# Moving the gate's exponentials on ScalarE, and the weights' lower half and the gating product on VectorE, in a projection stage

## The chip, the cores and the metric

The kernel runs on one core of a Trainium2 chip. Its time is the device time of one launch in microseconds; the median of three runs of the kernel before is 3620.22 us (3617.70 to 3620.62).

## What is computed

Two blocks follow each other on a sequence of 1024 tokens of width 1024: a gated MLP mixer and a dilated attention, then a block that mixes stick-breaking attention, a state-space recurrence (SSD) and a gated linear recurrence, and ends in an MLP. The change lies in the input projection of the second block, cut here to what matters:

```
h    = concat(16 meta tokens, x)                      # 1040 tokens
proj = rmsnorm(h) @ w_in                              # units of 128 features
xbc  = silu(causal_conv(proj[x,B,C], 4 taps) + bias)  # 8 units
z, q, g of the recurrences = silu(proj[z,q,g])        # 8 units
log_keep = log_sigmoid(-q k), summed from the right; w = exp(log_sigmoid(q k) + sum)
```

silu(y) is computed as y * exp(-ln(1 + exp(-y))), so that one activation table serves: ScalarE does Exp, Ln and Exp in place in one tile, `ce`, and VectorE multiplies.

## The kernel before

All matrix products of the projection are done in float32 by splitting each operand into a rounded upper part and a lower rest, and adding three products. ScalarE makes the upper half of a weight tile (`split_hi`, L137), VectorE the rest (`split_lo`, L142), and TensorE multiplies (`products`, L155) after it has waited for the lower half (`split`, L146).

`projection_and_sticks` (from L2492) works through 27 units of 128 output features, u = 0 to 26. A unit has three pieces, j = 0, 1, 2, of 352, 344 and 344 tokens (`PIECES`). Each piece has 8 groups of three matmuls into its own PSUM bank g[j]; TensorE may start piece (u, j) when VectorE has evicted piece (u-1, j). Weight tiles alternate between two buffers by u % 2. Units 7 to 14 go through the convolution (`is_x`), 15 to 22 only through silu (`is_silu`); both are "gated". Units 23 to 26 are stored raw.

The order of the work is written out by hand. `drive` calls, on every engine, `piece(p)` for p = 3u + j, `slot(c)` and `phase(k)`:

- pieces 6 to 14 (units 2 to 4) by themselves;
- 57 slots (c = -1 to 55) of stick-breaking attention. In slot c TensorE computes the scores of step c+1 (L2918, L2921), the sums of step c (L2931, L2933), the values of step c-1 (L2902), and then 6 or 7 groups of the projection, numbers 360c/56 to 360(c+1)/56. ScalarE and VectorE run the slot's own work first (ScalarE: L2767, L2769, L2771, then L2777, L2780, L2786; VectorE: L3103, L3112, L3117, L3121), and then the pieces that TensorE ends in that slot (units 5 to 19);
- 31 phases of the SSD recurrence, with the pieces of units 20 to 26 behind them in the same way.

Each engine works through its queue in order, so a wait in a piece holds up the next slot of that engine. Within `piece`, before the change:

- ScalarE: at j = 1 `split_hi` for the next unit, then (unit u-1 gated) a wait for VectorE's clamped tile (`s_cm`) and the first Exp (L2742); at j = 2 Ln (L2745) and the second Exp (L2747).
- VectorE: at j = 1 `split_lo` for the next unit; the eviction (L2996), which waits until TensorE has ended this piece; at j = 0 `finish(u-2)`, the gating product (L3011); then for unit u-1 two taps of the convolution at j = 0 (L3074, L3076), two more at j = 1 (L3080) and the clamp into `ce` (L3083; for silu units L3089 only). The clamp waits for the gating product of the unit before it.
- SyncE: at j = 1 the weights of unit u+2 are loaded (L132) and unit u-2 is stored (L2629).

Of the kernel before, what the change touches and what calls it, by code (L numbers as in the profile page):

```python
# [17 lines left out]
ACT = mybir.ActivationFunctionType  # L18
# [45 lines left out]
def wait(eng, sem, value):  # L64

    if isinstance(value, int) and value <= 0:
        return
    eng.wait_ge(sem, value)
# [2423 lines left out]
def projection_and_sticks(nc, a, w, hi, lo, inv, x, x_again, x_out, over_x, heads, hg, keep, table, cst, proj, conv, o_cat, ident, ones):  # L2492
# [10 lines left out]
    NU = len(units)  # L2503
# [5 lines left out]
    gated = lambda u: is_x(u) or is_silu(u)  # L2509
    n_gated = lambda u: u - 7  # L2510
# [13 lines left out]
    with Stage(nc, "pr") as st:  # L2524
# [17 lines left out]
        ce = st.sb("ce", [P, LM])  # L2542
# [152 lines left out]
        def _(act):  # L2695
# [20 lines left out]
            def root(u):  # L2716
                i = qk.index(u)
                act.wait_ge(s_pb, 3 * u + 3)
                nc.scalar.activation(cy[i % 2][:, :], cy[i % 2][:, :], ACT.Exp, scale=-0.5).then_inc(s_r, 1)

            def piece(p):
                u, j = p // 3, p % 3
                if j == 0 and u - 3 in qk:
                    root(u - 3)
                if j == 1 and u + 1 < NU:
                    w.split_hi(act, (u + 1) % 2, (u + 1) // 2, free=(s_mm, 3 * (u - 1) + 3))
                if u - 2 in qk:
                    i = qk.index(u - 2)
                    if j == 0:
                        act.wait_ge(s_ev, 3 * (u - 2) + 3)  # L2730
                        wait(act, s_blk, 3 * i)
                        nc.scalar.activation(ce[:, :], ev[(u - 2) % 3][:, TAPS - 1:], ACT.Square).then_inc(s_psq, 1)
                    c0, c1 = PIECES[j]
                    act.wait_ge(s_blk, 3 * i + j + 1)
                    if j == 0:
                        wait(act, s_nrm, i - 1)
                    nc.scalar.activation(cy[i % 2][:, c0:c1], pb[:, 0:c1 - c0], ACT.Ln, bias=eps[:, :], scale=1.0 / HD).then_inc(s_pb, 1)
                if gated(u - 1):
                    n = n_gated(u - 1)
                    if j == 1:  # L2740
                        act.wait_ge(s_cm, n + 1)
                        nc.scalar.activation(ce[:, :], ce[:, :], ACT.Exp, scale=-1.0).then_inc(s_cx, 1)  # L2742
                    if j == 2:
                        act.wait_ge(s_cx, n + 1)
                        nc.scalar.activation(ce[:, :], ce[:, :], ACT.Ln, bias=1.0).then_inc(s_cl, 1)  # L2745
                        act.wait_ge(s_cl, n + 1)
                        nc.scalar.activation(ce[:, :], ce[:, :], ACT.Exp, scale=-1.0).then_inc(s_ce, 1)  # L2747
                if (u, j) == (DT + 2, 0):
                    act.wait_ge(s_sdp, 64)
                    nc.scalar.activation(par[:, 2:3], par[:, 1:2], ACT.Exp).then_inc(s_dte, 1)  # L2750
                    act.wait_ge(s_dt, 2)
                    nc.scalar.activation(tmp, tmp, ACT.Exp, scale=-1.0).then_inc(s_dte, 1)
                    act.wait_ge(s_dte, 2)
                    nc.scalar.activation(tmp, tmp, ACT.Ln, bias=1.0).then_inc(s_dte, 1)
                if (u, j) == (DT + 4, 0):
                    act.wait_ge(s_dtc, 5)
                    for name in ("ecum", "wend", "elast"):
                        nc.scalar.activation(keep[name], keep["cum" if name == "ecum" else name], ACT.Exp).then_inc(s_dtx, 1)

            def slot(c):  # L2760
# [26 lines left out]
                for p in in_slot(c):  # L2787
                    piece(p)
# [28 lines left out]
            def phase(k):  # L2817
# [11 lines left out]
                if k == hg_from + 6:  # L2829
                    factors(0)  # L2830
            drive(act, piece, slot, phase)

        @block.tensor
# [117 lines left out]
        def _(dve):  # L2951
# [38 lines left out]
            def evict(u, j):  # L2990
                c0, c1 = PIECES[j]
                src = begin[u][j] if u < 2 else g[j]
                dve.wait_ge(s_mm, 3 * u + j + 1)
                if is_raw(u - 3):
                    dve.wait_ge(s_rawout[u % 3], 16 * raw_uses(u))
                nc.vector.tensor_tensor(ev[u % 3][:, TAPS - 1 + c0:TAPS - 1 + c1], src[:, 0:c1 - c0], inv[:, c0:c1], ALU.mult).then_inc(s_ev, 1)  # L2996
# [11 lines left out]
            def finish(u):  # L3008
                dve.wait_ge(s_ce, n_gated(u) + 1)
                src = cy[u % 2][:, :] if is_x(u) else ev[u % 3][:, TAPS - 1:]  # L3010
                nc.vector.tensor_tensor(cy[u % 2][:, :], src, ce[:, :], ALU.mult).then_inc(s_out, 1)  # L3011

            def piece(p):
                u, j = p // 3, p % 3
                if j == 1 and u + 1 < NU:
                    w.split_lo(dve, (u + 1) % 2, (u + 1) // 2)
                if j == 0 and u - 3 in qk:
                    i = qk.index(u - 3)
                    dve.wait_ge(s_scaled, 1)
# [2 lines left out]
                                                   cy[i % 2][:, :], ALU.mult, ALU.mult).then_inc(s_nrm, 1)  # L3022
                    dve.wait_ge(s_nrm, i + 1)
                evict(u, j)
                if (u, j) == (DT + 1, 1):
                    dve.wait_ge(s_kept, 16 * KT)
                    dve.wait_ge(s_sdp, 64)
                    dve.wait_ge(s_ev, 3 * u)
                    nc.vector.memset(dtf[:, 0:P - META], 0.0)
                    nc.vector.memset(tmp[:, 0:P - META], 0.0)  # L3030
                    nc.vector.tensor_scalar(dtf[:, P - META:], ev[DT % 3][0:SSD_HEADS, TAPS - 1:], par[:, 0:1], None, ALU.add).then_inc(s_dt, 1)
                    dve.wait_ge(s_dt, 1)
                    nc.vector.scalar_tensor_tensor(tmp[:, P - META:], dtf[:, P - META:], -1.0, dtf[:, P - META:], ALU.mult, ALU.max).then_inc(s_dt, 1)
# [17 lines left out]
                if u - 2 in vs:  # L3051
# [10 lines left out]
                            nc.vector.tensor_copy(vt[i][:, 4:8, :], src).then_inc(s_pb, 1)  # L3062
                    else:
                        nc.vector.tensor_copy(vt[i][:, 8, :], pb[:, 0:P]).then_inc(s_pb, 1)
                if j == 0 and gated(u - 2):
                    finish(u - 2)
                if is_x(u - 1):
                    v, n = u - 1, n_gated(u - 1)
                    src = ev[v % 3]
                    y = cy[v % 2][:, :]  # L3070
                    if j == 0:
                        wait(dve, s_gone[v % 2], 16 * (n // 2))
                        dve.wait_ge(s_ev, 3 * u)
                        nc.vector.tensor_scalar(y, src[:, 0:LM], taps[:, n, 0:1], cbias[:, n:n + 1], ALU.mult, ALU.add).then_inc(s_cc, 1)  # L3074
                        dve.wait_ge(s_cc, 4 * n + 1)
                        nc.vector.scalar_tensor_tensor(y, src[:, 1:1 + LM], taps[:, n, 1:2], y, ALU.mult, ALU.add).then_inc(s_cc, 1)  # L3076
                    if j == 1:
                        for t in (2, 3):
                            dve.wait_ge(s_cc, 4 * n + t)
                            nc.vector.scalar_tensor_tensor(y, src[:, t:t + LM], taps[:, n, t:t + 1], y, ALU.mult, ALU.add).then_inc(s_cc, 1)  # L3080
                        dve.wait_ge(s_cc, 4 * n + 4)
                        wait(dve, s_out, n)
                        nc.vector.tensor_scalar(ce[:, :], y, LOWEST, None, ALU.max).then_inc(s_cm, 1)  # L3083
                if is_silu(u - 1) and j == 1:
                    v, n = u - 1, n_gated(u - 1)
                    wait(dve, s_gone[v % 2], 16 * (n // 2))
                    dve.wait_ge(s_ev, 3 * u)
                    wait(dve, s_out, n)
                    nc.vector.tensor_scalar(ce[:, :], ev[v % 3][:, TAPS - 1:], LOWEST, None, ALU.max).then_inc(s_cm, 1)  # L3089

            def slot(c):
# [50 lines left out]
                for p in in_slot(c):  # L3142
                    piece(p)
# [41 lines left out]
            def phase(k):  # L3185
# [18 lines left out]
                if k == hg_from + 7:  # L3204
# [5 lines left out]
                    nc.vector.tensor_tensor(hg["kend"][0][:, :, :], hg["kend"][0][:, :, :], key[:, :, :], ALU.mult).then_inc(h_done, 1)  # L3210
                    dve.wait_ge(h_done, 1)
            drive(dve, piece, slot, phase)
    w.passed((14, 13), (0, 0))

# [935 lines left out]
```

## Time and profile before

| | |
|---|---|
| median of three runs | 3620.22 us (3617.70 to 3620.62) |
| the profiled execution | 3614.36 us |
| its span, first to last instruction | 3612.6 us |
| projection stage, units 2 to 26 | 2065 to 2598 us of the span |
| TensorE busy | 3451.5 us (96%) |
| VectorE busy | 2170.2 us (60%) |
| ScalarE busy | 1537.2 us (43%) |

Times in the rows are microseconds from the start of the span. A matmul's end is modelled: matmuls are pipelined, so in an unbroken run each starts about 0.16 us before the modelled end of the one before it. The idle time before an instruction stands in square brackets with what released it. TensorE's granted clock is given as a share of 2.4 GHz.

### The profile page before, as it was taken

Reading aid. Unit: us, or ns where it says so; the run is one execution under the profiler, and the core shown is the slowest. Engines: PE = TensorE matmul, PEld = TensorE weight load, DVE = VectorE, ACT = ScalarE, POOL = GpSimd, SP = SyncE. Lnnn points to the kernel's source line nnn. Section 1 sums busy time; section 2 is a strip of 40 time slices with the busy share of each in tenths; the row PEclk is TensorE's granted clock in tenths of the full one; section 3 lists DMA queues with packets and bytes.
Section 4 is the critical chain, followed back from the end, with each engine's and each line's share of the span. In section 5 each row is a group of like instructions: output and inputs, shape, how many; then the busy total and the mean of one; then the engine's idle time right before and its main releaser. Section 6 shows DMA issues by size and latency. Waiting matters only on the chain. (4 is left out here: it accounts for less than half of the span.)

```text
span 3612.6 us, 48153 instructions
## 1 busy us (share of the span) xinstructions
PE 3451.5 (96%) x17578; PEld 2817.6 (78%) x17578; DVE 2170.2 (60%) x4264; ACT 1537.2 (43%) x3062; POOL 121.9 (3%) x151
## 2 busy tenths in 40 slices
PE   8999999989999999999999799999879989999999
PEld 6878887867777777777777687778867877878887
DVE  5477773575555666666675646656666566644443
ACT  4254453445444454544444445555224322232222
POOL 0000001000000000000000200000000000000000
PEclk9999999999999999999999999999989999999999
DMA  4232225622111221222233300112232222322223
GB/s 147 94 106 92 88 91 187 193 68 62 59 59 55 65 66 63 68 65 64 67 100 123 124 28 32 50 56 77 96 108 91 96 86 72 108 93 94 99 94 123
DMA packets 162585, 316.84 MB, mean 88 GB/s; under 512 B 33744, under 2 KB 79360, under 8 KB 162224
## 3 DMA queue, kind: packets, MB, share of 16 engines
q1 hardware_dynamic: 144432, 268.49, 22.5%
q0 software_dynamic: 15808, 36.89, 3.3%
q10 hardware_dynamic: 2112, 8.39, 0.6%
q8 instruction: 142, 2.33, 0.3%
q14 instruction: 91, 0.75, 0.1%
HBM read 260.22 MB, written 59.71 MB: 89 GB/s over the span
## 5 line engine op out<-in xcount | busy, mean ns | idle before, releaser
L142 DVE TENSOR_TENSOR all_w_lo<-all_w_raw,all_w_hi 128x1024 fp32r<-128x1024 f32 x241 | 295.1, 1225 | 256.8 <-ACT all_w_hi L137 256.8
L137 ACT ACTIVATE all_w_hi<-all_w_raw 128x1024 fp32r<-128x1024 f32 x241 | 253.5, 1053 | 454.8 <-PE om_z L155 261.5
L155 PE MATMUL om_z<-all_hi,all_w_hi 128*128 128x512 f32 x640 | 256.9, 401 | 7.5 <-DVE all_w_lo L142 4.3
L155 PE MATMUL om_z<-all_hi,all_w_lo 128*128 128x512 f32 x640 | 255.1, 399 | 0.0
L155 PE MATMUL om_z<-all_lo,all_w_hi 128*128 128x512 f32 x640 | 253.6, 396 | 0.0
L2122 DVE CUSTOM_DVE_ANT_0 at_logit<-da_qk,at_bias 128x256 f32<-128x256 f32 (+1 forms) x384 | 130.1, 377 | 164.2 <-issue 163.6
L155 PE MATMUL pr_g<-all_hi,all_w_hi 128*128 128x344 f32 (+1 forms) x624 | 217.7, 349 | 11.4 <-PEq L45 4.9
L1668 ACT ACTIVATE at_p<-at_logit,da_pair_max 128x256 f32<-128x256 f32 (+1 forms) x384 | 177.5, 465 | 100.3 <-DVE da_pair_max L2122 100.3
L1660 ACT ACTIVATE at_pt<-da_tr 128x512 f32<-128x512 f32 (+1 forms) x192 | 101.2, 527 | 263.6 <-PE da_tr L1860 263.4
L155 PE MATMUL pr_g<-all_hi,all_w_lo 128*128 128x344 f32 (+1 forms) x624 | 206.4, 331 | 0.0
L155 PE MATMUL pr_g<-all_lo,all_w_hi 128*128 128x344 f32 (+1 forms) x624 | 205.2, 329 | 0.0
L155 PE MATMUL om_z<-om_h_hi,all_w_hi 128*128 128x512 f32 x512 | 202.3, 395 | 1.7 <-DVE all_w_lo L142 1.7
L155 PE MATMUL om_z<-om_h_lo,all_w_hi 128*128 128x512 f32 x512 | 200.1, 391 | 0.0
L155 PE MATMUL om_z<-om_h_hi,all_w_lo 128*128 128x512 f32 x512 | 200.0, 391 | 0.0
L3968 DVE TENSOR_TENSOR all_yo<-all_yo,om_z 128x512 f32<-128x512 f32 x80 | 55.0, 687 | 183.4 <-PE om_z L155 183.3
L1870 PE MATMUL da_pv<-at_v,at_pt 128*128 128x64 f32 x1280 | 164.1, 267 | 0.0
L1870 PEld LDWEIGHTS da_pv<-at_v,at_pt 128*128 128x128 f32 x1280 | 159.8, 192 | 1.9
L2139 DVE TENSOR_TENSOR da_o<-da_pv,da_rden 128x128 f32<-128x128 f32 x192 | 56.0, 292 | 167.4 <-PE da_pv L1870 161.8
L155 PEld LDWEIGHTS om_z<-all_hi,all_w_hi 128*128 128x128 f32 x640 | 121.9, 190 | 36.9 <-DVE all_w_lo L142 4.5
L1196 ACT ACTIVATE all_w_hi<-all_w_raw 128x512 fp32r<-128x512 f32 x190 | 118.3, 623 | 72.4 <-PE da_by L1214 23.8
L3863 ACT ACTIVATE om_h_hi<-om_m 128x512 fp32r<-128x512 f32 x64 | 40.4, 632 | 254.5 <-DVE om_m L3966 254.5
L155 PEld LDWEIGHTS om_z<-all_lo,all_w_hi 128*128 128x128 f32 x640 | 121.6, 190 | 27.8
(827 smaller groups left out, 8908.0 us busy)
## 6 DMA issues: line engine op xcount, KB each, us to landing
all_w_raw<-in_w_mlp SPq DMA_DIRECT2D x128, 512.0 KB, 3.4
all_w_raw<-in_w_qkv SPq DMA_DIRECT2D x136, 256.0 KB, 2.7
all_w_raw<-in_w_ug SPq DMA_DIRECT2D x48, 512.0 KB, 4.1
all_w_raw<-in_w_in SPq DMA_DIRECT2D x27, 512.0 KB, 3.5
all_w_raw<-in_w_v SPq DMA_DIRECT2D x20, 512.0 KB, 4.6
vhat<-ag_vst ACTq DMA_DIRECT2D x4, 2048.0 KB, 7.4
ow_v<-vhat SPq DMA_DIRECT2D x16, 512.0 KB, 3.4
da_before<-o_groups POOLq DMA_DIRECT2D x32, 256.0 KB, 3.9
```

What stands on the lines that cost most here:

```text
L137: self.nc.scalar.activation(self.hi[b][:, :], self.raw[b][:, :], ACT.Copy).then_inc(self.hi_done[b], 1)
L142: self.nc.vector.tensor_tensor(self.lo[b][:, :], self.raw[b][:, :], self.hi[b][:, :].bitcast(F32), ALU.subtract).then_inc(self.lo_done[b], 1)
L155: last = self.nc.tensor.matmul(out, wp[b][:, w], ap[:, k, cols], start=(k == 0 and m == 0), stop=(k == KT - 1 and m == 2))
L1196: self.nc.scalar.activation(self.hi[n % self.slots], self.tile[name], ACT.Copy, scale=self.scales[j] if name in ("a11", "a12") else 1.0).t ...
L1660: nc.scalar.activation(pt[t % 2][:, 0:wd], tr[:, 0:wd], ACT.Copy).then_inc(s_pt, 1)
L1668: last = nc.scalar.activation(p[t % 2][:, hh, 0:wd], logit[t % 2][:, hh, 0:wd], ACT.Exp, scale=-1.0, bias=pair_max[:, t, hh:hh + 1], accum ...
L1870: last = nc.tensor.matmul(pv[:, 64 * hh:64 * hh + 64], pt[t % 2][:, i * P:i * P + P], v[:, t + x, 64 * hh:64 * hh + 64], start=(x == 0), s ...
L2122: last = nc.vector.tensor_tensor_reduce(out=logit[t % 2][:, hh, 0:wd], in0=qk[hh][:, 0:wd], in1=bias[ag][hh][x][:, :], scale=1.0, scalar=3 ...
L2139: nc.vector.tensor_tensor(o[:, t, :].rearrange("p (h c) -> p h c", h=2), pv[:, 0:P].rearrange("p (h c) -> p h c", h=2), rden[:, t, :].rear ...
L3863: nc.scalar.activation(h_hi[:, i, :], m[n % 2][:, :], ACT.Square)
L3968: nc.vector.tensor_tensor(x[:, i, halves[h]], x[:, i, halves[h]], z[b][:, :], ALU.add).then_inc(s_ev, 1)
```

## The change

On ScalarE the first Exp moves from (u, 1) to (u, 2), where Ln follows it, and the second Exp from (u, 2) to (u+1, 0). On VectorE `split_lo` for the next unit moves from in front of the eviction of (u, 1) to behind the eviction of (u, 2), and in (u, 0) `finish(u-2)` moves behind the first two taps. No instruction is added or removed.

```
 scalar, piece(p):
-                if gated(u - 1):
+                if gated(u - 1) and j == 2:
                     n = n_gated(u - 1)
-                    if j == 1:
-                        act.wait_ge(s_cm, n + 1)
-                        nc.scalar.activation(ce[:, :], ce[:, :], ACT.Exp, scale=-1.0).then_inc(s_cx, 1)
-                    if j == 2:
-                        act.wait_ge(s_cx, n + 1)
-                        nc.scalar.activation(ce[:, :], ce[:, :], ACT.Ln, bias=1.0).then_inc(s_cl, 1)
-                        act.wait_ge(s_cl, n + 1)
-                        nc.scalar.activation(ce[:, :], ce[:, :], ACT.Exp, scale=-1.0).then_inc(s_ce, 1)
+                    act.wait_ge(s_cm, n + 1)
+                    nc.scalar.activation(ce[:, :], ce[:, :], ACT.Exp, scale=-1.0).then_inc(s_cx, 1)
+                    act.wait_ge(s_cx, n + 1)
+                    nc.scalar.activation(ce[:, :], ce[:, :], ACT.Ln, bias=1.0).then_inc(s_cl, 1)
+                if gated(u - 2) and j == 0:
+                    n = n_gated(u - 2)
+                    act.wait_ge(s_cl, n + 1)
+                    nc.scalar.activation(ce[:, :], ce[:, :], ACT.Exp, scale=-1.0).then_inc(s_ce, 1)
 vector, piece(p):
-                if j == 1 and u + 1 < NU:
-                    w.split_lo(dve, (u + 1) % 2, (u + 1) // 2)
...
                 evict(u, j)
+                if j == 2 and u + 1 < NU:
+                    w.split_lo(dve, (u + 1) % 2, (u + 1) // 2)
...
-                if j == 0 and gated(u - 2):
-                    finish(u - 2)
                 if is_x(u - 1):
...
+                if j == 0 and gated(u - 2):
+                    finish(u - 2)
                 if is_silu(u - 1) and j == 1:
```

## Rows read from the trace of the kernel before

**Rows 1.** The page: span, busy time by engine, clock in 40 slices.
```profile
span 3612.6 us, 48153 instructions
PE 3451.5 (96%) x17578; PEld 2817.6 (78%) x17578; DVE 2170.2 (60%) x4264; ACT 1537.2 (43%) x3062; POOL 121.9 (3%) x151
PEclk9999999999999999999999999999989999999999
```

**Rows 2.** Windows by stretch: length, each engine's busy time (instructions), clock, DMA share, GB/s.
```profile
2106.00:2181.00 75.00, 71.76 (x389) 58.02 (x388) 39.29 (x79) 44.88 (x89) 0.00 (x0) 0.98 0.07 24
2181.00:2390.00 209.00, 188.98 (x999) 153.91 (x999) 140.41 (x232) 120.11 (x223) 0.00 (x0) 0.92 0.12 41
2390.00:2475.00 85.00, 83.10 (x470) 68.59 (x468) 48.05 (x90) 54.61 (x99) 1.84 (x2) 0.99 0.19 66
2475.00:2598.00 123.00, 112.69 (x739) 109.98 (x738) 85.53 (x151) 41.91 (x78) 7.93 (x11) 0.99 0.27 91
```

**Rows 3.** TensorE's waits, 2106 to 2473 us: total us, times, longest.
```profile
PE pr_zb L2918 <- ACT pr_wt L2777: 17.4, 9, 3.7
PE pr_zb L2931 <- DVE ox_sticks L3121: 4.6, 6, 1.5
```

**Rows 4.** All waits, 2181 to 2390 us: ScalarE's longest.
```profile
ACT pr_ce L2742 <- DVE pr_ce L3083: 43.9, 8, 7.5
```

**Rows 5.** Timeline around the first of them: start, duration, engine, operation, idle before.
```profile
2200.80 1.07 ACT L2742 ACTIVATE pr_ce<-pr_ce 128x1040 f32<-128x1040 f32 x1 [7.53 <-DVE pr_ce L3083]
2202.94 0.26 ACT L2777 ACTIVATE pr_wt<-pr_zb 128x128 f32<-128x128 f32 x1
2203.26 1.22 PE L2918 MATMUL pr_zb<-hs_heads 64*128 64x384 f32 x2 [2.10 <-ACT pr_wt L2777]
```

**Rows 6.** TensorE's waits, 2473 to 2598 us.
```profile
PE pr_zb L2354 <- ACT pr_sp L2387: 3.5, 1, 3.5
```

**Rows 7.** Two lines, 2064 to 2598 us: count, duration in ns, min/median/max.
```profile
L142 DVE TENSOR_TENSOR all_w_lo<-all_w_raw,all_w_hi x25: 1202/1224/1226, 2063.6 to 2575.1; 128x1024 fp32r<-128x1024 f32 x25
L2996 DVE TENSOR_TENSOR pr_ev<-pr_g,all_inv x75: 491/516/527, 2071.6 to 2597.9; 128x344 f32<-128x344 f32 x50, 128x352 f32<-128x352 f32 x25
```

**Rows 8.** Timeline, start of unit 2.
```profile
2063.21 0.51 DVE L2996 TENSOR_TENSOR pr_ev<-pr_ob,all_inv 128x344 f32<-128x344 f32 x1
2063.63 1.22 DVE L142 TENSOR_TENSOR all_w_lo<-all_w_raw,all_w_hi 128x1024 fp32r<-128x1024 f32 x1
2064.95 0.63 PE L155 MATMUL pr_g<-all_hi,all_w_hi 128*128 128x352 f32 x1 [4.93 <-issue]
```

**Rows 9.** Timeline, end of unit 3 and start of unit 4.
```profile
2093.10 0.32 PE L155 MATMUL pr_g<-all_lo,all_w_hi 128*128 128x344 f32 x1
2093.46 0.52 DVE L2996 TENSOR_TENSOR pr_ev<-pr_g,all_inv 128x344 f32<-128x344 f32 x1 [3.84 <-PE pr_g L155]
2093.58 0.58 PE L155 MATMUL pr_g<-all_hi,all_w_hi 128*128 128x352 f32 x1
```

**Rows 10.** Timeline, end of unit 10: two groups' ends, next unit's start, eviction.
```profile
2253.02 0.32 PE L155 MATMUL pr_g<-all_lo,all_w_hi 128*128 128x344 f32 x1
2253.49 0.32 PE L155 MATMUL pr_g<-all_lo,all_w_hi 128*128 128x344 f32 x1
2253.65 0.32 PE L155 MATMUL pr_g<-all_hi,all_w_hi 128*128 128x352 f32 x1
2261.44 0.51 DVE L2996 TENSOR_TENSOR pr_ev<-pr_g,all_inv 128x344 f32<-128x344 f32 x1
```

**Rows 11.** Timeline of a slot in which nobody is late.
```profile
2183.75 1.03 PE L2918 MATMUL pr_zb<-hs_heads 64*16 64x512 f32 x2
2186.54 0.41 PE L155 MATMUL pr_g<-all_hi,all_w_hi 128*128 128x352 f32 x1
2188.36 0.67 DVE L3121 TENSOR_TENSOR ox_sticks<-pr_sp,pr_sp_hi 16x512 fp32r<-16x512 f32 x1
```

**Rows 12.** Windows from a gap on TensorE on: three of twelve.
```profile
2115.60:2121.80 6.20, 3.97 (x14) 3.69 (x14) 2.44 (x6) 2.59 (x5) 0.00 (x0) 0.73 0.00 0
2280.60:2286.80 6.20, 3.58 (x18) 2.48 (x19) 3.44 (x6) 5.92 (x11) 0.00 (x0) 1.00 0.01 3
2520.30:2528.00 7.70, 4.19 (x19) 4.17 (x19) 5.17 (x8) 3.59 (x4) 0.00 (x0) 0.78 0.20 68
```

## The prediction, made before the changed kernel was run

> **What bounds the kernel now.** I read the page first: TensorE is busy for 3451.5 of 3612.6 us at a clock near full [rows 1]. So the question for an edit on the other two engines is where TensorE waits. The change touches only units 2 to 26, so next come windows over that stage. While the convolution units run beside the sticks, from 2181 to 2390 us, TensorE is busy for 188.98 of 209 us at a clock of 0.92; in the silu units behind them for 83.10 of 85 us at 0.99 [rows 2]. There is something to win in the convolution units only.
>
> The waits say what. TensorE stands 17.4 us, 9 times, before the scores L2918, for ScalarE's weights L2777, and 4.6 us before the sums L2931, for VectorE [rows 3]. ScalarE in turn stands 43.9 us, 8 times, before the first Exp of the gate, until VectorE's clamp arrives [rows 4]; the next slot's work is queued behind that Exp. One instance: the Exp begins at 2200.80 after 7.53 us, L2777 follows at 2202.94, and TensorE resumes at 2203.26 after 2.10 us [rows 5]. In the SSD stretch the same wait of ScalarE holds up L2387, and TensorE stands 3.5 us for it [rows 6].
>
> **What the change removes.** With the first Exp one piece later, the clamp has been ready for a whole piece (some 7 us: a unit takes 209 / 8 = 26.1 us [rows 2]), so the wait of [rows 4] goes, and with it 17.4 us on TensorE [rows 3]. What may be late next is VectorE in (u, 1); but `split_lo` has left that piece, which makes it 1.22 us lighter [rows 7], so I count half of the 4.6 us as gained, 2.3. Of the 3.5 us [rows 6] I count 2.5, since the transposes that L2387 copies are only just done when the wait begins. Together 22 us (bounds: 12, if ScalarE's two operations together in (u, 2) make the next scores late instead, and 25.5, all of it).
>
> The clock comes back too. The two levels are 1.2 and 2.4 GHz. From 2106 to 2528 us TensorE has twelve gaps of 1.4 us or more. I opened a window at each, up to where the clock is full again: eight have a clock under 1 (0.73, 0.64, 0.76, 0.66, 0.77, 0.63, 0.65, 0.78), four stay at 1.00 (the first, a full one and the last are shown) [rows 12]. The window's length times what is missing to 1 is the time lost: 6.2 x 0.27 = 1.7 us in the first, 20.3 us over the eight, 2.5 us each. Seven of the eight follow a gap that goes: 19 us (bounds 10 and 19).
>
> **What the change adds.** `split_lo` for unit u+1 now stands behind the eviction of (u, 2), and that eviction waits until TensorE has ended (u, 2). TensorE can't begin (u+1, 0) before it. So a handover lies open at each of 24 unit boundaries, where there was none. The trace has the same handover once, where unit 2 starts: eviction at 2063.21, `split_lo` at 2063.63, first matmul at 2064.95 [rows 8], that is 1.74 us from the eviction's start to TensorE's. The eviction itself starts at best 0.04 us after the last matmul's end (2093.10 + 0.32, to 2093.46) when it has nothing else before it: there a small matmul for the norm lies between, and the next unit starts 0.16 us after the end [rows 9]. In an unbroken run it starts 0.16 us before the modelled end (2253.49 + 0.32, against 2253.65) [rows 10]. A bare handover thus costs 0.04 + 1.74 - 0.16 = 1.6 us, or 0.04 + 1.74 + 0.16 = 1.9 us.
>
> To that comes how late VectorE is. After unit 10 it evicts at 2261.44 what TensorE ended at 2253.81: 7.63 us late [rows 10]. Read in this way, the lags at the 24 boundaries (units 2 to 25) are 0.04, 0.04, 0.04; 0.15, 1.54, 1.26; 3.16, 3.21, 7.63, 1.03, 4.64, 3.64, 5.51, 0.04; 2.91, 2.92, 2.52, 0.04; 0.04, 0.04, 0.04, 0.26, 0.04, 2.02. Most of those in the convolution and silu units come from the wait that goes. What stays is the slot's own chain: in a slot without delay the scores start at 2183.75, the projection's groups at 2186.54, and VectorE is free at 2188.36 + 0.67 = 2189.03 [rows 11], 2.5 us after the groups began, or 2.5 - 0.47r where r groups of 0.47 us [rows 10] lie before the boundary. From the group numbers, the twelve boundaries inside a slot have r = 5, 3, 2; 5, 3, 1, 4, 3, 1; 6, 4, 2, so the lags add up to 12 us. The three boundaries that fall on a slot's end (after units 8, 12, 19), and the one after unit 4, have stick matmuls before the next unit, about 2.8 us [rows 11], and cost nothing.
>
> Stalls: two boundaries before the sticks at 1.6 = 3; three at 1.6 and nine at 1.9 inside the sticks = 22, with their lags 34; in the SSD stretch, where phase work lies between some pieces and I take gap and lag as they are in the trace, 1.6 + 1.4 + 0.4 + 0 + 1.9 + 1.9 = 7. Sum 44 us. Bounds: 32 with no lag at all, 66 with the lags of the trace as they stand.
>
> 18 of these are longer than 1.3 us. If two in three are followed by the low clock at 2.5 us each, as now [rows 12], that is 30 us (bounds: 0, and 45 if all are).
>
> **At nothing.** `finish` behind the two taps delays a store by some 2 us; nobody on TensorE's side reads it for over 10 us. The second Exp in (u+1, 0) ends before VectorE is through its eviction and taps. SyncE's load of unit u+2 now waits for a `split_lo` that ends a piece later, still before the point where the load is issued. If one of these covers failed it would be at most one operation of 1.1 us, eight times.
>
> **The sum.** 44 + 30 - 22 - 19 = +33 us. On the profiled execution, 3614.4 (span 3612.6 and 1.8 around it), that is 3647; it ran 5.9 us under the median, so against the median 3620.2 + 33 = 3653 us.
>
> A page bears on the third term. The Trainium skill, "TensorE: Matmul & The Clock Gate", section "HAM oscillation — how this bites in real kernels", describes a loop whose wait before every tile lets the clock fall every time, so that each tile starts cold. The trace agrees with it in part only: eight of twelve [rows 12].
>
> **The rivals.**
>
> - *Every handover pays the clock.* 44 + 45 - 41 = +48, 3668 us. For it: the stalls come with regularity and on top of the slot's own small gaps. Against: four gaps of 1.5 to 2.2 us have left the clock full. [...] Chance 0.10.
> - *VectorE stays late.* Lags as in the trace: 66 + 30 - 41 = +55, 3675 us. For it: VectorE has 140 of 209 us of work [rows 2] in strict order. Against: the 7.63 us is built on ScalarE's wait. Chance 0.10.
> - *An even trade.* The stalls are as long as forecast but the clock mostly stays up: 44 + 5 - 41 = +8 or less, around 3625. Chance 0.06.
> - *Faster.* ScalarE's wait was the dear part and the handover is bare: stalls 32, no low clock, all 41 (up to 44.5) back: -9 to -12, 3610 us. It decides if stall and lost clock together stay under 41 / 18 = 2.3 us a boundary. For it: 44 us of waiting in [rows 4] is the largest item in the stage. Against: the bare handover alone is 1.6 to 1.9. Chance 0.06.
> - The forecast, own range 3635 to 3665 us, has the other 0.68. That the change does not do what it says I exclude: the queues are in order and the waits are written out.
>
> **Range and chances.** From 3626 (just above the even trade) to 3683 (a late VectorE and the dear clock in part). Within 0.2%, 7 us, lies about what a measurement can tell from no change. Faster 0.06; same 0.07, from the even trade and the forecast's lower tail; slower 0.87.
>
> **What would show it.** ScalarE's wait before L2742 near zero; TensorE's before L2918 under 4 us; new waits of L155 for L142, 15 to 20 of them between 2065 and 2600 us, together near 44 us, longest after units whose boundary lies early in a slot (10, 11, 15, 18), absent after 4, 8, 12 and 19; more low clock from 2065 to 2600 us; the silu units, now at 0.99, worse than before; the convolution units about even. I am wrong if L155 hardly waits for L142, or if the convolution units gain more than the rest loses.

## The result, and the profile after

The changed kernel takes 3649.51 us (median of five, 3645.59 to 3652.46) against 3620.62 us (3617.70 to 3632.03) for the one before: the ratio is 1.0077 (95% interval 1.0061 to 1.0092). The medians are 28.9 us apart; the ratio gives 28 us. I had predicted 3653 us, in a range of 3626 to 3683. The profiled execution is the slowest of the five, 3652.46 us.

The page first; it is to be held against [rows 1]. TensorE's busy time is 25 us up, though it has the same instructions, and VectorE's and ScalarE's stand still:

```profile
span 3650.7 us, 48153 instructions
PE 3476.2 (95%) x17578; PEld 2834.2 (78%) x17578; DVE 2169.2 (59%) x4264; ACT 1539.2 (42%) x3062; POOL 122.1 (3%) x151
PEclk9999999999999999999999999889979999999999
```

Then the windows by stretch, as in [rows 2] (length; busy time of TensorE, its weight loads, VectorE, ScalarE, GpSimd; clock, DMA share, GB/s), with the units before the sticks in the first:

```profile
2065.30:2106.00 40.70, 38.35 (x214) 36.36 (x215) 9.63 (x15) 9.25 (x12) 0.00 (x0) 0.93 0.13 40
2106.00:2185.00 79.00, 71.87 (x391) 58.21 (x389) 38.99 (x80) 42.23 (x84) 0.00 (x0) 0.98 0.07 22
2185.00:2395.00 210.00, 190.74 (x997) 154.79 (x997) 139.41 (x231) 120.45 (x219) 0.00 (x0) 0.91 0.12 41
2395.00:2503.00 108.00, 97.80 (x499) 79.12 (x497) 50.18 (x96) 58.70 (x105) 1.84 (x2) 0.89 0.16 52
2503.00:2623.00 120.00, 111.35 (x732) 107.44 (x731) 82.85 (x143) 42.31 (x77) 7.67 (x10) 1.00 0.28 95
```

The convolution units, in the third row, are as long as before and lose about the same to the clock. The silu units, in the fourth, were the clean ones at 0.99; they are now at 0.89. Read unit by unit, from each unit's first matmul to the next one's, the stage divides like this (us):

| units | 2-4 | 5-7 | 8-15 | 16-19 | 20-26 | stage |
|---|---|---|---|---|---|---|
| before | 44.6 | 71.6 | 208.9 | 86.6 | 118.3 | 530.1 |
| after | 47.7 | 79.1 | 208.6 | 103.3 | 119.2 | 557.8 |

The stage is 27.7 us longer. The other 10 us of the two spans' difference lie behind it: 7 in the recurrence stage that follows, where the clock of this execution was lower (0.72 against 0.80), and 3 in the rest. In the executions of the experiments the time from the projection's last matmul to the first of the next big stage runs from 106.0 to 115.7 us, and the kernels do the same work there. So I compare the length of the projection stage, from the first matmul of unit 2 to the start of the last of unit 26, below.

TensorE's waits from 2065 to 2624 us, against [rows 3] and [rows 6] (total us, times, longest):

```profile
PE pr_g L155 <- DVE all_w_lo L142: 40.3, 20, 4.8
PE pr_ob L2342 <- DVE ox_ab L2409: 2.7, 2, 2.2
PE pr_zb L2354 <- ACT pr_sp L2387: 0.7, 1, 0.7
PE pr_pb L2372 <- DVE pr_wt L2442: 0.6, 1, 0.6
```

The wait for the lower half is new. The 17.4 us before L2918 and the 4.6 us before L2931 are gone altogether, and 3.5 us before L2354 have become 0.7. The longest of the new waits stands at the end of unit 10, the boundary of [rows 10]; here are both engines' timelines:

```profile
2258.62 0.31 PE L155 MATMUL pr_g<-all_lo,all_w_hi 128*128 128x344 f32 x1
...
2260.62 0.69 DVE L3121 TENSOR_TENSOR ox_sticks<-pr_sp,pr_sp_hi 128x512 fp32r<-128x512 f32 x1
2261.23 0.42 DVE L3127 TENSOR_TENSOR pr_o<-pr_o,pr_orr 128x256 f32<-128x256 f32 x1
2261.68 0.43 DVE L3129 TENSOR_TENSOR pr_o<-pr_o,pr_og 128x256 f32<-128x256 f32 x1
2262.02 0.51 DVE L2996 TENSOR_TENSOR pr_ev<-pr_g,all_inv 128x344 f32<-128x344 f32 x1
2262.45 1.22 DVE L142 TENSOR_TENSOR all_w_lo<-all_w_raw,all_w_hi 128x1024 fp32r<-128x1024 f32 x1
...
2263.72 0.66 PE L155 MATMUL pr_g<-all_hi,all_w_hi 128*128 128x352 f32 x1 [4.79 <-DVE all_w_lo L142]
2264.18 0.49 PE L155 MATMUL pr_g<-all_hi,all_w_lo 128*128 128x352 f32 x1
```

TensorE ends the unit at 2258.93. VectorE is still in the slot's own work until 2262.02, 3.09 us later (it was 7.63 before), then evicts and splits, and TensorE goes on at 2263.72: 3.09 + 1.70, and the next matmuls take 0.49 us in place of 0.32, at the lower clock. At the end of unit 9 VectorE is not late, and the handover is bare; two small matmuls still lie in the gap, so the idle time in brackets is less than the 1.74 us between the units:

```profile
2235.96 0.52 DVE L2996 TENSOR_TENSOR pr_ev<-pr_g,all_inv 128x344 f32<-128x344 f32 x1
2236.39 1.22 DVE L142 TENSOR_TENSOR all_w_lo<-all_w_raw,all_w_hi 128x1024 fp32r<-128x1024 f32 x1
...
2237.67 0.43 PE L155 MATMUL pr_g<-all_hi,all_w_hi 128*128 128x352 f32 x1 [1.34 <-DVE all_w_lo L142]
```

The account of the stage, in us, with the clock's share as length times what is missing to 1 in the window rows: waits for L142 +40.3; waits gone 17.4 + 4.6 + 2.8 + 0.8 (L2372) = -25.6; clock 32.4 against 20.3, +12. The sum is +27, measured +27.7.

### The profile page after: what moved, and what is told of

It is laid out like the page before. It is cut to its first block and busy times, and to the rows that moved or that the text cites. A ratio compares the mean times of both kernels' runs of the same rounds, so it can differ in the third digit from the quotient of the medians.

```text
span 3650.7 us, 48153 instructions
## 1 busy us (share of the span) xinstructions
PE 3476.2 (95%) x17578; PEld 2834.2 (78%) x17578; DVE 2169.2 (59%) x4264; ACT 1539.2 (42%) x3062; POOL 122.1 (3%) x151
## 5 line engine op out<-in xcount | busy, mean ns | idle before, releaser
L142 DVE TENSOR_TENSOR all_w_lo<-all_w_raw,all_w_hi 128x1024 fp32r<-128x1024 f32 x241 | 294.9, 1224 | 243.2 <-ACT all_w_hi L137 243.2
L155 PE MATMUL pr_g<-all_hi,all_w_hi 128*128 128x344 f32 (+1 forms) x624 | 219.7, 352 | 51.5 <-DVE all_w_lo L142 40.3
L155 PE MATMUL om_z<-all_hi,all_w_hi 128*128 128x512 f32 x640 | 258.1, 403 | 7.7 <-DVE all_w_lo L142 4.6
L155 PE MATMUL om_z<-all_hi,all_w_lo 128*128 128x512 f32 x640 | 256.5, 401 | 0.0
L155 PE MATMUL om_z<-all_lo,all_w_hi 128*128 128x512 f32 x640 | 254.8, 398 | 0.0
L155 PE MATMUL pr_g<-all_hi,all_w_lo 128*128 128x344 f32 (+1 forms) x624 | 207.8, 333 | 0.0
L155 PE MATMUL pr_g<-all_lo,all_w_hi 128*128 128x344 f32 (+1 forms) x624 | 206.9, 332 | 0.0
L155 PE MATMUL om_z<-om_h_hi,all_w_hi 128*128 128x512 f32 x512 | 202.3, 395 | 1.7 <-DVE all_w_lo L142 1.7
L155 PE MATMUL om_z<-om_h_lo,all_w_hi 128*128 128x512 f32 x512 | 200.1, 391 | 0.0
L155 PE MATMUL om_z<-om_h_hi,all_w_lo 128*128 128x512 f32 x512 | 200.0, 391 | 0.0
L155 PEld LDWEIGHTS pr_g<-all_hi,all_w_hi 128*128 128x128 f32 x624 | 124.0, 199 | 61.8 <-DVE all_w_lo L142 47.0
L155 PEld LDWEIGHTS om_z<-all_hi,all_w_hi 128*128 128x128 f32 x640 | 122.7, 192 | 37.5 <-DVE all_w_lo L142 4.8
L1196 ACT ACTIVATE all_w_hi<-all_w_raw 128x512 fp32r<-128x512 f32 x190 | 118.3, 623 | 72.9 <-PE da_by L1214 23.8
```

The source lines that it names most:

```text
L142: self.nc.vector.tensor_tensor(self.lo[b][:, :], self.raw[b][:, :], self.hi[b][:, :].bitcast(F32), ALU.subtract).then_inc(self.lo_done[b], 1)
L155: last = self.nc.tensor.matmul(out, wp[b][:, w], ap[:, k, cols], start=(k == 0 and m == 0), stop=(k == KT - 1 and m == 2))
L1196: self.nc.scalar.activation(self.hi[n % self.slots], self.tile[name], ACT.Copy, scale=self.scales[j] if name in ("a11", "a12") else 1.0).t ...
```

## The experiments

Each was timed beside the kernel before, in three groups, in which its medians were 3620.77, 3625.57 and 3621.84 us; a ratio is to the kernel before of the same group. In a diff, `split_lo` stands for the two lines of the condition and the call.

**The lower half's move alone.**

```
 kernel before, vector, piece(p):
-                if j == 1 and u + 1 < NU: split_lo
                 evict(u, j)
+                if j == 2 and u + 1 < NU: split_lo
```

> The kernel before with one edit: split_lo stands behind the eviction of (u, 2), as in the changed kernel; ScalarE's exponentials and the gating product stay where they were. Theory (the handover is the whole cost, and ScalarE's move the whole gain): VectorE's lags stay, since ScalarE still waits for the clamp, but the waits before L2918 fall behind a stall and shrink; stalls of L155 for L142 near 60 us in 20 or more waits, about 3675 us, slower than the changed kernel by 20 to 30 us. Rival A (ScalarE's move gives nothing once the handover is there): the same as the changed kernel, 3650 us. Rival B (ScalarE's move costs something itself): faster than the changed kernel, 3635 us.

Measured: 3671.80 us (3666.64 to 3677.51), ratio 1.0140 (1.0121 to 1.0160). Its waits (TensorE, 2100 to 2570 us):

```profile
PE pr_g L155 <- DVE all_w_lo L142: 47.1, 16, 7.9
PE pr_zb L2918 <- ACT pr_wt L2777: 5.1, 4, 2.1
```

Over the stage it is 51.5 us in 20 waits, and the stage is 587.5 us, 57 longer than before. That is the theory's time. The wait for ScalarE before L2918 has shrunk from 17.4 to 5.1 us without any edit there, though ScalarE still waits 35 us for the clamps of the convolution units: the stall in front of it gives ScalarE the time. So the new stall buys back old waits, which is why its price can't be added to them as they stand. On the kernel before, the lower half's move costs 51 us; on top of ScalarE's edit, where there are no such waits left to buy back, it costs 65 us (the next experiment).

**The lower half put back.**

```
 changed kernel, vector, piece(p):
+                if j == 1 and u + 1 < NU: split_lo
                 evict(u, j)
-                if j == 2 and u + 1 < NU: split_lo
```

> The changed kernel with split_lo put back to (u, 1) in front of its eviction; ScalarE's exponentials and the gating product stay moved. Theory: no L155 waits for L142, the 17.4 us before L2918 are gone and most of the 4.6 before L2931, and the clock falls seldom from 2180 to 2400 us: 22 to 26 us of waits and 15 to 19 of clock, about 3580 us. Rival (VectorE is late in (u, 1) as before, with 5 us of work there, and TensorE then waits before L2931 for it instead): 3600 to 3620 us.

Measured: 3584.32 us (3579.30 to 3586.66), ratio 0.9897 (0.9882 to 0.9913), 65 us under the changed kernel. Its waits and windows in the sticks and behind them:

```profile
PE pr_zb L2931 <- DVE ox_sticks L3121: 4.9, 4, 1.5
```

```profile
2106.00:2446.00 340.00, 331.85 (x1861) 271.35 (x1859) 227.02 (x401) 220.71 (x408) 1.85 (x2) 0.98 0.14 47
2446.00:2563.00 117.00, 112.34 (x738) 109.85 (x738) 82.74 (x144) 42.47 (x77) 7.37 (x10) 0.99 0.27 93
```

There is no wait for L142. The 4.9 us before L2931 stay, where I had expected most of the 4.6 to go. The stage is 497.2 us, 33 us shorter than before, and the clock loses 8 us of these two windows in place of 20.3.

**ScalarE's part alone.** The kernel before with the ScalarE hunk of the change only; the gating product stays in front of the taps.

> The kernel before with the ScalarE edit alone: first Exp and Ln in (u, 2), second Exp in (u+1, 0); VectorE's order is that of before, with the gating product in front of the taps. Theory: as e2 within 5 us, near 3583 us, since VectorE waits about 1 us per unit for the second Exp in (u, 0), hidden beside TensorE. Rival (the gating product in front of the taps now holds up VectorE, and the taps, clamp and next slot behind it): 10 us or more slower than e2, 3595 us.

Measured: 3585.58 us (3583.12 to 3593.08), ratio 0.9901 (0.9884 to 0.9917); stage 496.1 us, 4.9 us before L2931. That is within 2 us of the kernel with the lower half put back, whose only other difference is the gating product's place. So that place is worth nothing that shows, and the whole gain of the change is ScalarE's edit.

**The lower half in the last piece, but in front of the eviction.**

```
 changed kernel, vector, piece(p):
+                if j == 2 and u + 1 < NU: split_lo
                 evict(u, j)
-                if j == 2 and u + 1 < NU: split_lo
```

> The changed kernel with split_lo still in (u, 2), but in front of the eviction instead of behind it, so that it no longer waits for TensorE's end of the piece; one pair of lines swapped. Theory: the eviction's wait is all that makes split_lo late. TensorE's 40.3 us for L142 go except where VectorE is later than the whole piece; 3575 to 3585 us, as e2 or up to 5 us better, since (u, 1) is lighter. Rival (the place in the last piece is too late in any case, since VectorE is some us behind TensorE): waits of L155 for L142 of 10 us or more stay, 3595 us or more.

Measured: 3615.26 us (3608.99 to 3626.53), ratio 0.9988 (0.9976 to 1.0000). My expectation failed and the rival held. The waits (TensorE, 2100 to 2570 us), and the end of unit 10, which TensorE reaches at 2254.01:

```profile
PE pr_g L155 <- DVE all_w_lo L142: 25.7, 13, 4.4
```

```profile
2255.70 0.69 DVE L3121 TENSOR_TENSOR ox_sticks<-pr_sp,pr_sp_hi 128x512 fp32r<-128x512 f32 x1
2256.30 0.42 DVE L3127 TENSOR_TENSOR pr_o<-pr_o,pr_orr 128x256 f32<-128x256 f32 x1
2256.76 0.42 DVE L3129 TENSOR_TENSOR pr_o<-pr_o,pr_og 128x256 f32<-128x256 f32 x1
2257.10 1.22 DVE L142 TENSOR_TENSOR all_w_lo<-all_w_raw,all_w_hi 128x1024 fp32r<-128x1024 f32 x1
```

`split_lo` waits for nothing here, and comes at 2257.10 all the same: it stands in the queue behind the slot's work, with which VectorE is up to 3.1 us behind TensorE's end of the unit, here as in the changed kernel. I had taken the semaphore for the cause. Inside the sticks the place in the queue is more than half of it: of the changed kernel's 33.4 us of these waits 25.7 stay, and units 5 to 19 take 368.7 us, against 391.0 in the changed kernel and 337.3 with the lower half put back. In units 20 to 26, where VectorE is not behind, this place costs nothing (115.5 us against 115.3 with the lower half put back).

**Behind an eviction, but a piece earlier.**

```
 changed kernel, vector, piece(p):
                 evict(u, j)
-                if j == 2 and u + 1 < NU: split_lo
+                if j == 1 and u + 1 < NU: split_lo
```

> The changed kernel with split_lo behind the eviction of (u, 1) instead of (u, 2): it still waits for TensorE's end of a piece, but of one that lies a whole piece ahead of the boundary. Theory (what costs is only that there is no piece of cover left, not that split_lo waits behind an eviction): no waits of L155 for L142 worth more than 1 us together, 3580 to 3590 us, as with split_lo in front of that eviction. Rival (VectorE's lag in the sticks eats the piece too, as it did in the kernel with split_lo in front of the last eviction): 5 to 15 us of such waits, 3595 us or more.

Measured: 3585.64 us (3582.00 to 3589.29), ratio 0.9903 (0.9885 to 0.9921); stage 495.3 us, no wait for L142 among TensorE's. Waiting for an eviction is harmless when a whole piece of TensorE's work lies between.

**The handover in units 20 to 26 only.** As the kernel with the lower half put back, with `split_lo` at j = 2 behind the eviction when u + 1 is 20 or more.

> As the kernel with the lower half put back (3584 us), but for units 20 to 26 split_lo stands behind the eviction of (u, 2): seven bare handovers in the SSD stretch, where VectorE is not late and some stalls of the same length lie there anyway. Theory: 0.2 + 1.6 + 1.3 + 0.4 + 0 + 1.9 + 0.9 = 6 us from the gaps of the changed kernel less those of before, no low clock from them: 3590 us. Rival (two in three of them also lose 2.5 us of clock, as my prediction had it): 3600 us.

Measured: 3593.42 us (3581.70 to 3600.39), ratio 0.9916 (0.9895 to 0.9938). Its row of waits for L142 and its last window:

```profile
PE pr_g L155 <- DVE all_w_lo L142: 4.6, 4, 1.7
```

```profile
2454.00:2574.00 120.00, 111.34 (x721) 107.65 (x720) 81.29 (x141) 42.06 (x77) 7.68 (x10) 0.99 0.28 95
```

Units 20 to 26 take 120.8 us against 115.3 (113.8 in that kernel's second trace, below): 5.5 to 7 us, and the stage 502.0 against 497.2 and 494.8. The bare handover has its price here, and no low clock comes with it that the kernel without it hasn't also (0.99 in both). The medians differ by 9 us, but their ranges overlap and they are of different groups; units 5 to 19 are the same in the traces (336.9 against 337.3 us), so the stage is the better measure.

**Work in the stalls.**

```
 changed kernel, tensor, piece(p), at j == 0:
+                        if 11 <= u < 20:
+                            for _ in range(7):
+                                nc.tensor.matmul(pb[:, :], hi[:, 0, 0:P], hi[:, 0, 0:HALF], start=True, stop=True)
                         w.split(pe, u % 2, u // 2)
```

> The changed kernel; on TensorE, in front of the wait for the lower half of units 11 to 19, seven matmuls of 512 columns more, whose result nobody reads, about 0.23 us each, so that 1.6 us of each of these nine stalls are worked through. The handover itself stays. Theory (the stall itself and the clock it lets fall are two costs): L155's waits for L142 shrink by 1.6 us each on paper, but the next unit starts when it did; the clock between 2250 and 2500 us is lost for 10 us or less instead of some 30, and the time falls to 3630 to 3640 us. Rival (the clock falls for another reason than these stalls, or filling them costs as much as it saves): 3648 to 3655 us.

Measured: 3623.86 us (3614.89 to 3643.75), ratio 1.0005 (0.9988 to 1.0022). The waits from 2100 to 2570 us, the windows over the sticks and behind them, and the added matmuls (count, ns of one, first and last start):

```profile
PE pr_g L155 <- DVE all_w_lo L142: 21.7, 13, 3.2
```

```profile
2108.00:2485.00 377.00, 353.78 (x1943) 286.44 (x1943) 230.57 (x408) 223.98 (x413) 1.85 (x2) 0.98 0.13 44
2485.00:2603.00 118.00, 109.35 (x709) 105.66 (x708) 79.38 (x137) 40.06 (x73) 7.69 (x10) 0.99 0.27 93
```

```profile
L2857 PE MATMUL pr_pb<-all_hi x63: 387/389/476, 2259.7 to 2459.1; 128*128 128x512 f32 x63
```

Over the whole stage the waits are 26.2 us; with nine fillings of 1.6 us that is 40.6, the 40.3 of the changed kernel. So the handovers are as long as they were. But the clock loses 377 x 0.02 + 118 x 0.01 = 8.7 us in place of 32.4, and the stage is 539.5 us long in place of 557.8. Adding 14 us of useless work to TensorE saves 18 us of the stage, and the launch is 26 us faster than the changed kernel, each held against the kernel before of its group; I had expected 10 to 20. So the stall and the clock are two costs. In the changed kernel a stretch of low clock follows seven of these nine stalls; with the filling it follows one of them, for 3.4 us from 2433.6 us on, where TensorE still stands 2.1 us behind the added matmuls.

**A version that beats both.** With the lower half in (u, 1), what stays in the sticks is VectorE's 5 us of work in that piece. A three-way split of it, on top of the kernel with the lower half put back:

```
 vector, for unit u-1: taps 0 and 1 at j == 0; clamp at j == 2
-                    if j == 1:
-                        for t in (2, 3): tap t
+                    if j: tap j + 1
-                if j == 0 and gated(u - 2): finish(u - 2)
+                if j == 1 and gated(u - 2): finish(u - 2)
 scalar:
-  Exp and Ln of unit u-1 at j == 2, second Exp of unit u-2 at j == 0
+  Exp and Ln of unit u-2 at j == 0, second Exp of unit u-2 at j == 1
```

> The kernel with the lower half put back (3584 us), with VectorE's work of a convolution unit spread over three pieces: taps 0 and 1 in (u, 0), tap 2 and the gating product in (u, 1), tap 3 and the clamp in (u, 2); Exp and Ln follow in (u+1, 0), the second Exp in (u+1, 1). Theory (the 4.9 us that TensorE still waits before L2931 come from the 5 us that VectorE has to do in (u, 1)): these go, and with them one fall of the clock: 3577 to 3581 us. Rival (VectorE's lateness there comes from the slots themselves): 3583 to 3587 us, no difference.

Measured: 3578.10 us (3575.26 to 3585.75), ratio 0.9885 (0.9865 to 0.9906). In the sticks:

```profile
PE pr_zb L2931 <- DVE ox_sticks L3122: 0.5, 1, 0.5
```

```profile
2105.00:2441.00 336.00, 332.26 (x1887) 272.86 (x1886) 229.03 (x406) 221.22 (x409) 1.85 (x2) 0.99 0.14 48
```

Units 8 to 15 take 174.0 us in place of 180.9 and the stage 489.6 in place of 497.2. Both kernels once more, side by side:

> The kernel with the lower half put back, once more, to stand on the same chip as the three-way split. Theory: 3580 to 3590 us, 30 to 40 us faster than before.

> The three-way split once more, beside the kernel it is compared with. Theory: 3575 to 3580 us, 5 to 8 us faster than the kernel with the lower half put back, since its stage is 7.6 us shorter in the traces (489.6 against 497.2 us). Rival (that difference was one of the two executions): within 3 us of it.

Measured: 3583.65 us (3580.49 to 3583.97) and 3578.55 us (3574.05 to 3586.01), stages 494.8 and 489.7 us. The medians are 5 us apart both times, but the ranges overlap; that the stage is 5 to 8 us shorter is in both pairs of traces, that the launch is faster by as much is likely and not shown.

## Why the prediction was right

The forecast was +33 us; the stage is 27.7 us longer and the launch 28.9. Point by point, by its own steps:

- *What bounds the stage.* Right, and the two single edits show it apart: ScalarE's alone takes the stage from 530.1 to 496.1 us, the lower half's alone to 587.5. Together they would give +23 us of the stage if they did not meet; measured is +28.
- *Waits removed, 22 us.* 25.6 measured, or 24.8 without L2372, which the prediction doesn't count. Its "some 7 us" for a piece should be 8.7, a third of 26.1; nothing hangs on it. Of the 4.6 before L2931 I had kept half as late VectorE; in the changed kernel all went, with `split_lo` out of (u, 1). With it back in (u, 1) they stay, 4.9.
- *Clock back, 19 us.* With the lower half put back the sticks lose 340 x 0.02 = 7 us, and before they lost 19 in the first three windows of [rows 2]: 12 us, inside the bounds of 10 to 19 and below my value. I had seven of the eight stretches of low clock go; in the trace with the lower half put back three are left, after a wait of 2.25 us before L2884, of 1.54 us before L2931 and of 2.17 us before L2342. The first and the last are waits that the change doesn't touch.
- *The handover, 1.6 to 1.9 us, at all boundaries but three or four.* 20 waits. Ten boundaries of the changed kernel show 1.74 us between the units' matmuls, where before seven of the ten lay between a gap of 0.20 and an overlap of 0.20.
- *VectorE's lag.* I took 12 us for the slot's own chain. At the twelve boundaries inside a slot it is 0.14, 1.53, 1.26; 0.04, 3.09, 1.71, 0.04, 2.32, 0.04; 0.13, 1.98, 1.26 us, 13.5 in all. The sum came out, but the single places did not, and that they make up for each other is luck. The rule gives 1.1, 2.0 and 2.0 us after units 10, 11 and 15, where 3.09, 1.71 and 0.04 were measured, and 1.1 and 0.6 after 14 and 17, where 2.32 and 1.98 were. It took one chain of 2.5 us, from a slot with operations 512 wide, for every slot. The slot in which unit 15 ends is 128 wide, and VectorE is through it before TensorE ends the unit:

```profile
2398.21 0.29 DVE L3121 TENSOR_TENSOR ox_sticks<-pr_sp,pr_sp_hi 128x128 fp32r<-128x128 f32 x1 [0.55 <-ACT pr_sp_hi L2786]
2398.95 0.52 DVE L2996 TENSOR_TENSOR pr_ev<-pr_g,all_inv 128x344 f32<-128x344 f32 x1 [0.46 <-PE pr_g L155]
```

So the waits are longest after units 10, 14, 17 and 11, and not after 10, 11, 15 and 18 as forecast. Another place was off: at the ends of units 8 and 12, which fall on a slot's end, TensorE did wait (0.66 and 0.48 us), since VectorE was 0.90 and 1.24 us late.
- *The stalls' sum, 44 us.* 40.3 of idle time. Counted as the prediction does, as the gap between two units' matmuls less that of before, it is 44 us over the boundaries other than 8 and 12, and 1.1 at these two.
- *The new stalls' clock, 30 us.* The changed kernel loses 32.4 us in these windows, some 31 of it in falls after the first of [rows 12]. The size was right and its spread was not: I had two in three of 18 stalls pay 2.5 us. In fact the bare handovers of units 20 to 26 pay nothing (1.00 in the last window), and in the sticks the clock falls after seven of fourteen waits and loses 31 us, more than 4 us a fall. Fewer falls and dearer ones made up for each other, which is luck too. The Trainium skill ("TensorE: Matmul & The Clock Gate", "HAM oscillation — how this bites in real kernels") describes a loop in which a DMA wait of some 3 to 5 us before every tile lets the clock fall each time. It does not say so of waits as short as the bare handover. The trace agrees in part: all five waits of 2.96 us or more in the sticks go with low clock, two of the nine shorter ones there do, and none of the four behind the sticks, the longest of which is 1.74 us. The filled stalls show, for nine of them, that the clock falls because TensorE stands still.
- *Where it would show.* As forecast: the convolution units about even (208.9 and 208.6), the silu units worse (86.6 and 103.3), ScalarE's wait for the convolution's clamp gone. A part of the wait for the silu clamp stays in the SSD stretch (11.5 us, twice), and TensorE doesn't stand for it. After unit 4 there is no wait of L155 (3.26 us lie between the units in both kernels), and after unit 19 there are 1.74 us in place of 1.59, which is as good as nothing.
- *The rivals.* "Faster" needed stall and lost clock together under 2.3 us a boundary; 40.3 and 31 us over 20 waits are 3.6. It had the bare price in its 32 us of stalls, and fell by the lags and the clock. "An even trade" fell by the clock alone; its sum, +8, is 3628 us and not 3625. "VectorE stays late" is what the lower half's move alone showed, 3672 us, and ScalarE's edit is what cured it.

## What to carry to other kernels

When an operation that feeds the next tile is moved behind the last thing that waits for the present tile, a pipeline becomes a handover: its price is that operation's chain plus however late its engine is, at every tile. One piece of the consumer's work between the two is enough to hide it, even behind a wait; being free of the wait is not enough when the queue in front is late. And split a change of several edits before judging it: here one half was worth -35 us, and the other +51 us alone and +65 us on top of the first.

## What the runs showed of the hardware

Filling nine stalls of TensorE with 63 matmuls that nobody reads made the stage 18 us shorter, since the clock then lost 8.7 us and not 32.4.

In the changed kernel seven of fourteen waits for the lower half in the sticks go with low clock (its start lies within 2 us of the wait's end), which loses 31 us in all, and none of four in the SSD stretch. The length of the wait goes with it, but does not settle it: five of the seven are the five waits of 2.96 us or more, while 1.74 us was enough at 2340.6 us and not at 2400.7. The wait of 2.65 us after unit 6 was followed by no low clock in the changed kernel and by 6.8 us of it in the kernel with the filling, which is the same up to there. So whether a single wait costs clock differs from one execution to the next.

The SSD stretch has one wait as long as 1.74 us in the changed kernel, and in the kernel with the handover there alone, and neither is followed by low clock. TensorE's work is dense between its handovers, and in the sticks there are small gaps besides; that this makes a difference is argued, not shown. What the chip wants of a stretch to hold the clock was not measured here.
